# State-space scan: four masked diagonal blocks in one PSUM bank, two blocks without a mask, and the backward exponentials of the second tile in two activations

## What is computed

```
z, xbc, dt_raw = split(h @ w_in)
xbc = silu(depthwise_conv(xbc))                  # width 5, centred
xs, Bm, Cm = split(xbc)                          # 32 heads of 64; 8 groups, state 128
dt = softplus(dt_raw + dt_bias)                  # forward and backward, per head
A = -exp(a_log)
y_fwd = ssd_chunked(xs, dt[fwd], A[fwd], Bm, Cm)
y_bwd = flip(ssd_chunked(flip(xs), flip(dt[bwd]), A[bwd], flip(Bm), flip(Cm)))
y = y_fwd + y_bwd + xs * d_skip
y = group_rms_norm(y * silu(z)) @ w_out
```

## Time and profile before

| | |
|---|---|
| median of three runs | 1990.55 us (1990.10 to 1992.21) |
| the profiled execution | 1990.11 us |
| span from its first to its last instruction | 1988.3 us |
| around the span | 1.8 us |
| TensorE busy | 1879.2 us, 95% |
| VectorE busy | 1427.2 us, 72% |
| ScalarE busy | 1175.5 us, 59% |
| mean granted TensorE clock | 0.979 |
| the scan (start of its first matmul to the release of the last output) | 1138.5 us to about 1205.3 us |

### The profile page before, as it was taken

One profiled execution on the slowest core, in us unless ns is written; L12 is line 12 of the kernel. 1 busy time (PEld: TensorE's weight loads), 2 busy tenths in 40 slices (PEclk: granted clock), 3 DMA queues, 4 the chain that ended last, 5 costly groups with the idle time before them and its releaser, 6 DMA issues.

```text
span 1988.3 us, 36076 instructions
## 1 busy us (share of the span) xinstructions
PE 1879.2 (95%) x14638; PEld 1729.2 (87%) x14638; DVE 1427.2 (72%) x2196; ACT 1175.5 (59%) x2092; POOL 12.8 (1%) x25
## 2 busy tenths in 40 slices
PE   8898999898989998999999999999989999989998
PEld 7887999797779997999889867899989998879998
DVE  5687777754677778877778676877787777575555
ACT  6545656655666566665676675655565555574332
POOL 0000000020000000000000000000000000000000
PEclk9999999999999998999999999999999999999999
DMA  8304666354056664888334402687768773224551
GB/s 327 116 4 149 233 238 221 131 179 154 33 208 245 227 236 168 315 296 292 131 128 168 162 1 86 269 300 278 265 235 304 277 275 117 86 96 160 190 191 54
DMA packets 96358, 374.98 MB, mean 189 GB/s; under 512 B 5825, under 2 KB 6465, under 8 KB 95425
## 3 DMA queue, kind: packets, MB, share of 16 engines
q1 hardware_dynamic: 95552, 372.15, 51.7%
q10 hardware_dynamic: 640, 0.52, 0.1%
HBM read 371.08 MB, written 1.05 MB: 187 GB/s over the span
## 4 chain that ended last, share of the span: by engine, by line
PE 82%; DVE 9%; ACT 6%; issue 3%; ACTq 0%; DMA 0%; DVEq 0%; SPq 0%
PE psum L1093 36%; PE psum L1109 16%; PE psum L774 8%; PE psum L867 4%; PE psum L1074 2%; DVE buf L670 2%; PE psum L595 2%; DVE htok L3007 1%; PE psum L732 1%; PE psum L1723 1%; PE psum L3116 1%; PE psum L3575 1%; DVE x_res L530 1%; PE psum L2609 1%; DVE htok L529 1%
## 5 line engine op out<-in xcount | busy, mean ns | idle before, releaser
L1093 PEld LDWEIGHTS psum<-buf,buf 128*128 128x128 f32 x6048 | 741.2, 192 | 8.9
L1093 PE MATMUL psum<-buf,buf 128*128 128x256 f32 x6048 | 744.5, 283 | 0.0
L1109 PE MATMUL psum<-buf,buf 128*128 128x512 f32 x1584 | 381.9, 391 | 0.0
L1109 PEld LDWEIGHTS psum<-buf,buf 128*128 128x128 f32 x1584 | 289.6, 188 | 55.4 <-DVE buf L1158 0.3
L988 DVE TENSOR_TENSOR buf<-ring,buf 128x1024 fp32r<-128x1024 f32 x264 | 310.5, 1219 | 8.7 <-DVE modT L1044 7.5
L982 ACT ACTIVATE buf<-ring 128x1024 fp32r<-128x1024 f32 x264 | 262.5, 1044 | 0.0
L774 PE MATMUL psum<-buf,buf 128*128 128x256 f32 x1944 | 244.7, 285 | 9.2 <-DVE buf L670 8.5
L774 PEld LDWEIGHTS psum<-buf,buf 128*128 128x128 f32 x1944 | 236.4, 191 | 15.4 <-DVE buf L670 13.9
L1004 DVE TENSOR_TENSOR buf<-ring,buf 128x1024 fp32r<-128x1024 f32 x132 | 161.6, 1224 | 86.7 <-ACT buf L999 86.7
L999 ACT ACTIVATE buf<-ring 128x1024 fp32r<-128x1024 f32 x132 | 139.4, 1056 | 85.2 <-PE psum L1109 82.7
L1127 ACT ACTIVATE htok<-psum 128x256 f32<-128x256 f32 x88 | 33.8, 384 | 235.0 <-PE psum L1093 226.9
(11 more groups left out here) (431 smaller groups left out, 2068.2 us busy)
## 6 DMA issues: line engine op xcount, KB each, us to landing
ring<-in_w_ffn SPq DMA_DIRECT2D x88, 1536.0 KB, 7.0
buf<-in_w_mod SPq DMA_DIRECT2D x144, 512.0 KB, 4.6
ring<-in_w_conv SPq DMA_DIRECT2D x44, 1536.0 KB, 6.6
ring<-in_w_ssd_in SPq DMA_DIRECT2D x16, 1536.0 KB, 6.5
ring<-in_w_ns_in SPq DMA_DIRECT2D x7, 1536.0 KB, 7.5
ring<-in_w_hy_in SPq DMA_DIRECT2D x6, 1536.0 KB, 15.0
ring<-in_w_ssd_out SPq DMA_DIRECT2D x5, 1536.0 KB, 6.8
ring<-in_w_cmp SPq DMA_DIRECT2D x4, 1024.0 KB, 5.1
```

What stands on the lines that cost most here:

```text
L1093: ins = E.matmul(b[:, g * T:(g + 1) * T], w[:, wa, g, k, :], h[:, ha, k, :], start=k + n_ == 0, stop=k == KC - 1 and n_ == 2)
L1109: ins = E.matmul(acc[:, t, g * 512:(g + 1) * 512], hr[z][:, ha, t * P:(t + 1) * P], wd[j][:, wa, g * 512:(g + 1) * 512], start=j == 0 and ...
```

## The change

`rows(h)` has three matmuls in place of four. The mask table has four blocks, the forward and backward triangles in turn, so that the first bank holds the four diagonal blocks, all masked (blocks 0 to 3). The second bank gets the two off-diagonal blocks (4: tile 0 backward, 5: tile 1 forward) from the `acT` matmul alone. The mask table is made by four copies, in place of a memset and three copies.

`exponentials(h)` has five activations in place of four. The two forward exponentials with the bias of tile 0 (blocks 0 and 5) are read in one activation of 256 columns, with a stride that reaches from one bank into the other. The two backward ones with the bias of tile 1 (blocks 4 and 3) lie in PSUM in the opposite order to that in `ee`, and are two activations of 128 columns. Where the results lie in `ee`, and all that follows, is as before. From L3036 on, line numbers in the new file are smaller by up to one.

```
-            masks = ar.take(5 * P, F32R)
+            masks = ar.take(4 * P, F32R)
...
-                V.memset(whole(masks[:, P:3 * P]), 0.0)
-                for a, name in ((0, "neg_f"), (3, "neg_b"), (4, "neg_f")):
-                    ins = V.tensor_copy(masks[:, a * P:(a + 1) * P], cst(name))
+                for a in range(4):
+                    ins = V.tensor_copy(masks[:, a * P:(a + 1) * P], cst(("neg_f", "neg_b")[a % 2]))
...
-                    E.matmul(X[q][:, 0:512], idr, masks[:, 0:512], start=True, stop=False)
+                    E.matmul(X[q][:, 0:512], idr, masks, start=True, stop=False)
                     E.matmul(X[q][:, 0:512], one_head, acT, start=False, stop=True)
-                    E.matmul(X[q][:, 512:768], idr, masks[:, 384:640], start=True, stop=False)
-                    ins = E.matmul(X[q][:, 512:768], one_head, acT[:, 128:384], start=False, stop=True)
+                    ins = E.matmul(X[q][:, 512:768], one_head, acT[:, 128:384], start=True, stop=True)
...
-                x4 = X[h % 2][:, 0:512].rearrange("p (a n) -> p a n", a=4)
+                block_of = lambda a: X[h % 2][:, a * P:(a + 1) * P]
+                forward = X[h % 2][:, 0:768].rearrange("p (a n) -> p a n", a=6)[:, 0:6:5, :]
...
-                    A.activation(two_of(0), x4[:, 0:4:2, :], ACT.Exp, bias=by(0, 0))
-                    A.activation(two_of(256), x4[:, 1:4:2, :], ACT.Exp, bias=by(1, 1))
-                    A.activation(e[:, 512:640], X[h % 2][:, 512:640], ACT.Exp, bias=by(0, 1))
-                    x_free[h] = act.count(A.activation(e[:, 640:768], X[h % 2][:, 640:768], ACT.Exp,
-                                                       bias=by(1, 0)).then_inc(act.sem, 1))
+                    A.activation(two_of(0), forward, ACT.Exp, bias=by(0, 0))
+                    A.activation(e[:, 256:384], block_of(4), ACT.Exp, bias=by(1, 1))
+                    A.activation(e[:, 384:512], block_of(3), ACT.Exp, bias=by(1, 1))
+                    A.activation(e[:, 512:640], block_of(1), ACT.Exp, bias=by(0, 1))
+                    x_free[h] = act.count(A.activation(e[:, 640:768], block_of(2), ACT.Exp, bias=by(1, 0)).then_inc(act.sem, 1))
```

## The result

Over 19 executions of each kernel, the changed kernel's median is 1995.9 us (1991.1 to 1998.2) and that of the kernel before 1991.5 us (1989.4 to 1996.2). The ratio is 1.0016, with a 95% interval of [1.0009, 1.0023]: about 3.2 us slower (the medians alone are 4.4 us apart). The forecast was 1991.2 us in a range of 1989.2 to 1993.5, so the time lies outside of it. Both kernels spread over some 7 us, more than the first three times had shown.

What follows compares the result with a forecast made beforehand. The prediction took a circle of activations, rows and sums in the scan as the bound. Terms +2.24, -1.68, +0.05 and +0.10 summed to +0.7 us: 1990.11 became 1990.8, median forecast 1991.2 us, range 1989.2 to 1993.5.

Steps and rivals of the forecast that it cites:

- circle: In the scan, one head's activations, rows and sums wait for each other in a loop, 3.93 us each time round.
- R: One head's rows on TensorE: 0.12 us shorter by the removed matmul, over 14 heads -1.68 us.
- first rival: Removed matmul was covered and gives 0, so the split's cost stands alone: +2.6 us, 1993.1 us; 13%.
- link E: One head's activations on ScalarE: 0.14 us longer by the split, over 16 heads +2.24 us.
- turn: One pass of the scan's loop, two heads: 3.93 us before, to stay at 3.93 to 3.97 us.
- scan's balance: Sum of the forecast's gains and costs in the scan: +0.7 us.
- second rival: TensorE is the engine that counts in the scan: 28 x 0.12 = -3.4 us, 1987.2 us; 6%.
- third rival: TensorE's clock falls in the scan as its idle time grows: half of 13 turns at half clock, +10 us, 2001 us; 4%.
- sign of being wrong: In the scan: turn under 3.85 or over 4.05 us, wide activation over 0.50 us, or clock falling between 1138 and 1205 us.
- Start and end: Scan's edges: first three heads' activations add 3 x 0.14 us, head 0's earlier start 0 (bound -0.24), last products +0.10 us.
- Beside the circle: In the scan, the second head's extra 0.14 us on ScalarE is hidden; TensorE's second removed matmul is worth nothing.

Runs made afterwards that it cites:

- pair_swapped: Changed kernel with the second tile's two backward exponentials in one forward-reading activation, leaving blocks 3 and 4 exchanged in `ee`; ratio to the kernel before 0.9990.
- reversed: Changed kernel with the second tile's two backward exponentials in one activation stepping backwards from block 4 to 3, result right; ratio to the kernel before 0.9983.
- split_only: Kernel before with L3086 alone split into two activations of 128 columns, all four matmuls kept; ratio to the kernel before 1.0031.
- again: Changed kernel without an edit, run once more for its trace; ratio to the kernel before 1.0016.
- again2: Changed kernel without an edit, run a third time; ratio to the kernel before 1.0020.
- shift25: Kernel before with eleven unused 512-column matmuls ahead of `rows(16)`, in the middle of the scan; ratio to the kernel before 1.0027.
- filled: Changed kernel with six unused 512-column matmuls behind `rows(1)`, in the idle time before `rows(2)`; ratio to the kernel before 0.9999.
- shift09: Kernel before with four unused 512-column matmuls ahead of `rows(16)`, in the middle of the scan; ratio to the kernel before 0.9997.
- filled_shift: Changed kernel with six unused matmuls behind `rows(1)` and nine ahead of `rows(16)`; ratio to the kernel before 1.0012.

## Why the prediction was wrong

- **The circle and its links: right, a little too cheap.** R fell by 0.12 us (0.90 to 0.78), and `pair_swapped` and `reversed`, which have that part alone, gave -1.6 for the -1.7 of the sum. The split cost 0.14 us in the starts, and `split_only` gave +2.5 where the first rival's arithmetic has 2.6 for the same term (of which it gives 0.35 without a working). The link E as a whole, from L3084 to the next L3064, went from 1.40 (1154.48 to 1155.88 before) to 1.56 us, so the turn went from 3.93 to 3.97, where I had 3.95. With the full clock the scan's balance was +1.0 us for a forecast +0.7.
- **The first and second rivals: out.** The removed matmul was not covered, and TensorE's saved time off the circle only became idle time.
- **The third rival: right in kind, wrong in place and in weight.** I looked for a fall of the clock in the turns. There TensorE idled for 0.26 us of each turn before and for 0.55 with the edit (I had 0.6 and 0.9), was still busy for 0.86 of the time, and in no trace did the clock fall between two turns. The clock falls at the start, just behind the wait between `rows(1)` and `rows(2)`. My sign of being wrong, a fall between 1138 and 1205 us, came true.
- **The step that failed** is the item *Start and end*, with the one *Beside the circle*. The first priced the start by what the edit does to the chain (3 x 0.14, bound -0.24); the second called TensorE's saved matmuls worth nothing. The forecast was a sum over links, with no term for the clock after a longer wait. In the traces that wait went from 1.41 us of idle time after 1.63 of work to 1.79 after 1.41, and the scan lost 2.0 us by 6.8 us at half clock. 1.64 us of idle time after 1.41 of work, and 1.56 after 1.63, left the clock as it was. So in the traces it took both halves of the edit. I had given the rival 4% at 10 us.
- **The rule of the Trainium skill** (TensorE: Matmul & The Clock Gate, A second HAM failure mode: psum-queue depth-cycling) had pointed to the short idle times of such a loop. The scan's turns don't bear it out, at idle times of 0.26 to 0.55 us a turn; the fall came behind one longer wait at the loop's start.
- **What the sum left out altogether**: the 780 us behind the scan. I let the scan's balance pass through one to one. In the traces, they changed by +0.9 and +0.8 (`again`, `again2`), +3.6 (the first trace of the changed kernel), +4.4 (`split_only`, `shift25`), -0.6 (`filled`, `shift09`) and -1.8 us (the shorter scans). In `again` the parts are 1.0 of links, 2.0 of the scan's clock and 0.9 behind the scan, together 3.9 us beside the 3.2 by the ratio.
- **The range**: I had three times within 2.1 us and took their spread for that of the kernel. The median of the kernel before is 1991.5 us over 19 executions, 0.9 above the one that I started from; 35 times of the kernel before, in the last batch, reach from 1989.2 to 1999.4 us.

What stays open: why the first trace of the changed kernel has 787.3 us behind its scan and the other two 784.5. The difference arises for the most part near 1700 us, where the first has a stretch of 6.8 us at half clock (from 1699.1) and the other two have none; why is not known. Nor is it settled why `filled_shift` came out 5 us shorter behind its scan than the first trace of the changed kernel, with scans that differ by 0.1 us.

It was not tried how long the idle time at the scan's start may be before the clock falls in most executions; three traces with 1.79 us had it, and seven with 1.41 to 1.64 had not. These are not ten separate trials: in all of them the last half-clock stretch ahead stands at the same distance from the scan. The three traces of the changed kernel are of executions of 1995.1 to 1997.8 us. Of the 19 of the comparison, 13 took 1994.6 to 1998.2 us at a mean granted clock of 0.974 to 0.977, and six took 1991.1 to 1994.0 at 0.979 to 0.980. No trace shows one of the six, so it is not known whether the clock fell at their scan's start.

## What to carry to other kernels

When an edit takes work from TensorE while it waits for another engine anyway, look at the longest wait near it and not only at the loop: work that was worthless on the chain may have helped to keep the clock up, and a few unused matmuls put into that wait show whether it did. Before a link is taken away and another made longer for it, look for a form that needs no second instruction; here a negative stride did what two activations did, and the same edit turned from 0.16% slower into 0.17% faster. And where a span has many half-clock stretches, a difference of one to three microseconds in one stage can bring another -2 to +4 behind it, so compare such kernels by the stage that was edited, and test the rest with a plain delay of the same length.

## What the hardware showed that I had not expected

- The granted clock fell at a place that is tied to the program: in all 14 traces the last half-clock stretch ahead of the scan began 170.6 to 170.8 us before the scan's first matmul (read in steps of 0.1 us), although that matmul itself came between 1138.5 and 1142.4 us after the start of the span.
- An idle time of 1.8 us, behind 1.4 us of matmuls at the full clock, was followed by 6.8 us at 1.2 GHz in all three traces of the changed kernel. The fall was recorded 0.1 to 0.3 us after TensorE had started again (1142.7, 1143.2 and 1145.9 us, for matmuls that started at 1142.56, 1142.89 and 1145.64). It cost the scan only 2.0 us: at the full clock TensorE was busy for 4.62 of 6.60 us there (`filled`), and at half clock for 6.43.
- An activation that reads PSUM with one stride across two banks (0.47 us; in `reversed` 486 ns on average), and one that steps backwards (487 ns), cost what a stride within one bank had cost (486 and 487 ns).
